# Rotary queries transposed by VectorE, the short weight tiles' low parts made by GpSimd, and scores one tile later

## What is computed

```python
q = (rms_norm(c_q, norm_cq) @ w_uq).reshape(B, S, MLA_HEADS, QK_NOPE + QK_ROPE)   # 16 heads, 128 + 64
q = jnp.concatenate([q[..., :QK_NOPE], apply_rope(q[..., QK_NOPE:], cos, sin)], axis=-1)
kv = (rms_norm(c_kv, norm_ckv) @ w_ukv).reshape(B, S, MLA_HEADS, QK_NOPE + V_HEAD)
k = jnp.concatenate([k_nope, jnp.broadcast_to(k_r, ...)], axis=-1)
o = chunk_causal_attention(q, k, v, (QK_NOPE + QK_ROPE) ** -0.5)
...
merged = jax.nn.sigmoid(gate_a) * y_a + jax.nn.sigmoid(gate_b) * y_b
x = x + merged @ w_o[l]
x = x + memory_cross_attention(rms_norm(x, norm_cross[l]), mem_n, ...)
x = x + swiglu(rms_norm(x, norm_ffn[l]), w_gate[l], w_up[l], w_down[l])
```

## Time and profile before

| what | value |
|---|---|
| median of 3 runs | 1653.96 us (1653.91 to 1654.84) |
| the profiled execution | 1653.59 us |
| its span, first to last instruction | 1651.8 us |
| mean granted TensorE clock | 0.998 |
| TensorE (PE) busy | 1640.0 us, 99% |
| TensorE weight loads (PEld), beside the products | 1372.2 us, 83% |
| VectorE (DVE) busy | 1199.7 us, 73% |
| ScalarE (ACT) busy | 812.0 us, 49% |
| GpSimd (POOL) busy | 105.2 us, 6% |

### The profile page before, as it was taken

One profiled execution on the slowest core, in us unless ns is written; L12 is line 12 of the kernel. 1 busy time (PEld: TensorE's weight loads), 2 busy tenths in 40 slices (PEclk: granted clock), 3 DMA queues, 4 the chain that ended last, 5 costly groups with the idle time before them and its releaser, 6 DMA issues.

```text
span 1651.8 us, 23135 instructions
## 1 busy us (share of the span) xinstructions
PE 1640.0 (99%) x7708; PEld 1372.2 (83%) x7708; DVE 1199.7 (73%) x1670; ACT 812.0 (49%) x1040; POOL 105.2 (6%) x154
## 2 busy tenths in 40 slices
PE   9999999999999999999999999999999999999998
PEld 7888888888888888888888888888888888888886
DVE  5678998899988877888668766666666666654454
ACT  7556554555444544555555544444444444344343
POOL 3100111120000000120002100000000000000000
PEclk9999999999999999999999999999999999999999
DMA  6875655555566675655435666666666666665564
GB/s 232 257 203 169 178 155 166 170 164 179 164 187 204 202 230 169 200 195 175 151 116 192 199 195 191 191 192 193 194 193 184 186 202 197 195 218 180 186 212 135
DMA packets 161408, 309.86 MB, mean 188 GB/s; under 512 B 10272, under 2 KB 16928, under 8 KB 161088
## 3 DMA queue, kind: packets, MB, share of 16 engines
q1 hardware_dynamic: 159152, 302.03, 59.7%
q0 software_dynamic: 1488, 6.42, 1.1%
q10 hardware_dynamic: 704, 0.58, 0.1%
HBM read 306.89 MB, written 2.10 MB: 187 GB/s over the span
## 4 chain that ended last, share of the span: by engine, by line
PE 98%; issue 0%; ACT 0%; DMA 0%; DVE 0%; SPq 0%; POOLq 0%; POOL 0%; ACTq 0%; DVEq 0%
PE acc L370 30%; PE acc L372 29%; PE acc L371 29%; PE tp L382 1%; PE sc L531 1%; PE acc L611 1%; PE acc L613 1%; PE acc L612 1%; PE ov L510 0%; PE sc L526 0%; DMA xs<-in_x_dram 0%; PE sc L499 0%; PE acc L460 0%; PE acc L461 0%; PE acc L462 0%
## 5 line engine op out<-in xcount | busy, mean ns | idle before, releaser
L1431 DVE TENSOR_TENSOR w_lo<-raw,w_hi 128x1024 fp32r<-128x1024 f32 (+3 forms) x591 | 719.5, 1222 | 345.8 <-ACT w_hi L856 337.9
L856 ACT ACTIVATE w_hi<-raw 128x1024 fp32r<-128x1024 f32 (+3 forms) x591 | 605.6, 1027 | 732.1 <-PE acc L372 681.8
L370 PE MATMUL acc<-w_hi,crossT 128*128 128x512 f32 x832 | 324.4, 390 | 0.2 <-ACTq L1119 0.2
L371 PE MATMUL acc<-w_lo,crossT 128*128 128x512 f32 x832 | 323.8, 389 | 0.0
L372 PE MATMUL acc<-w_hi,crossT 128*128 128x512 f32 x832 | 323.8, 389 | 0.0
L370 PE MATMUL acc<-w_hi,mixT 128*128 128x512 f32 x732 | 289.1, 395 | 1.4 <-DVE mixT L1642 1.2
L372 PE MATMUL acc<-w_hi,mixT 128*128 128x512 f32 x732 | 285.1, 390 | 0.0
L371 PE MATMUL acc<-w_lo,mixT 128*128 128x512 f32 x732 | 285.1, 389 | 0.0
L370 PEld LDWEIGHTS acc<-w_hi,crossT 128*128 128x128 f32 x832 | 156.2, 188 | 33.3 <-DVE w_lo L1431 0.5
L372 PEld LDWEIGHTS acc<-w_hi,crossT 128*128 128x128 f32 x832 | 156.2, 188 | 32.5
L371 PEld LDWEIGHTS acc<-w_lo,crossT 128*128 128x128 f32 x832 | 156.2, 188 | 32.0
(11 more groups left out here) (291 smaller groups left out, 1605.5 us busy)
## 6 DMA issues: line engine op xcount, KB each, us to landing
raw<-in_w_in_dram SPq DMA_DIRECT2D x104, 512.0 KB, 3.7
raw<-in_w_gate_dram SPq DMA_DIRECT2D x88, 512.0 KB, 4.3
raw<-in_w_up_dram SPq DMA_DIRECT2D x88, 512.0 KB, 3.7
raw<-in_w_down_dram SPq DMA_DIRECT2D x80, 512.0 KB, 4.6
raw<-in_w_kv_mem_dram SPq DMA_DIRECT2D x64, 512.0 KB, 3.7
raw<-in_w_o_dram SPq DMA_DIRECT2D x32, 512.0 KB, 4.4
raw<-in_w_q_mem_dram SPq DMA_DIRECT2D x32, 512.0 KB, 4.4
raw<-in_w_o_mem_dram SPq DMA_DIRECT2D x32, 512.0 KB, 4.0
```

The costliest lines, as they stand in the source:

```text
L370: mm(o, lo, whi, start=first and k == 0, stop=False)
L371: mm(o, hi, wlo, start=False, stop=False)
L856: fn(w_hi[:, s, 0:width], raw[:, s, 0:width], ACT.Copy).then_inc(hi_done, 1)
L1431: V.tensor_tensor(w_lo[:, s, 0:width], raw[:, s, 0:width], w_hi[:, s, 0:width].bitcast(F32), ALU.subtract).then_inc(lo_done, 1)
```

## The change

- TensorE no longer transposes rotary queries in the first seven pairs (`rotary_turned` is gone, and `rotary_out` on ScalarE). VectorE does it in 16 more transposes of 32 partitions by 64 elements, eight at step 3 and eight at step 4, behind a wait for `rope_ready`; the last of them now raises `q_turned`.
- The low parts of tiles 8 to 11 of every pair are made by GpSimd (`short_tiles_lo`, ahead of the rope). VectorE leaves its four splits out, waits for GpSimd's semaphore `pool_lo` one step later (steps 5 to 8), and raises `lo_done` in its place, so that `lo_done` is still counted in order.
- Values and scores stand after tile 7, not after tile 6; the masking and the gating on VectorE move to steps 7 and 8.
- The taps are shared out anew over the steps; their number is the same.
- Memory group 2 is made at step 10 of the last pair, not at step 11, on ScalarE ahead of the exponentials.
- GpSimd computes the memory's row factor after the first pair's rope.

```diff
-            def rotary_turned(p, q):
-                pe.wait_ge(rope_ready, p + 1)
-                for b in range(NB):
-                    turn_group(q, b, [qr_tok[:, b, :, :].rearrange("p h d -> p (h d)")])
...
-                if t == (4 if last else 6):
+                if t == (4 if last else 7):
                     if nth > 1:
                         values(i - 2, v_pair[parity], nth == 2)
-                    scores(i - 1, i + (Q_C - 1), nth == 1, last)
+                    scores(i - 1, nth == 1, last)
...
-            def rotary_out(p, q, first):
-                if not first:
-                    act.wait_ge(scores_ready, 2 * p)
-                for b in range(NB):
-                    act.wait_ge(turned, 2 * q + (b + 1))
-                    fn(qrT[:, b * P:(b + 1) * P], tp[:, b, 0:P], ACT.Copy).then_inc(turned_out[b], 1)
...
-                    if last and t == 11:
+                    if last and t == 10:
                         act.wait_ge(tile_done, i * 12 + (T_C + 8))
                         operand_hi(2)
...
             def query_turn(n):
-                i, j = n // 4, n % 4
+                i, j = n % 16 // 4, n % 4
+                if n >= 16:
+                    src = qr_tok[32 * i:32 * i + 32, :, j // 2, 32 * (j % 2):32 * (j % 2) + 32]
+                    to = qrT[32 * j:32 * j + 32, :].rearrange("p (b t) -> p b t", b=NB)
+                    ins = V.transpose(to[:, :, 32 * i:32 * i + 32], src)
+                    if n == 31:
+                        ins.then_inc(q_turned, 1)
+                    return
...
-                if t == (4 if last else 6):
+                if t == (4 if last else 7):
                     masked_scores(i - 1, nth == 1)
-                if t == (5 if last else 7) and nth > 1:
+                if t == (5 if last else 8) and nth > 1:
                     gate_values(i - 2)
...
-            share = [0, 1, 3, 5, 8, 10, 12, 12, 13, 16, 18, 19, EARLY_TAPS]
+            share = [0, 1, 3, 5, 6, 7, 9, 12, 12, 15, 18, 19, EARLY_TAPS]
-            share_last = [0, 1, 3, 5, 9, 12, 15, 15, 16, 17, 18, 19, EARLY_TAPS]
-            turn_now = {0: (7, 10), 1: (10, 13), 2: (13, 16)}
+            share_last = [0, 1, 3, 5, 6, 7, 9, 12, 12, 15, 18, 19, EARLY_TAPS]
+            turn_now = {0: (7, 10), 1: (10, 13), 2: (13, 16), 3: (16, 24), 4: (24, 32)}
...
-                    split_lo(i * 12 + T_C, t + 4, width)
+                    if t in (5, 6, 7, 8):
+                        dve.wait_ge(pool_lo, 4 * i + (t - 4))
+                        dve.sem_inc(lo_done, 1)
+                    if t not in (4, 5, 6, 7):
+                        split_lo(i * 12 + T_C, t + 4, width)
...
-                    if last and t == 11:
+                    if last and t == 10:
                         operand_lo(2)
...
+                    if t == 3 and not first:
+                        dve.wait_ge(rope_ready, i)
...
+            def short_tiles_lo(p):
+                for t, n in ((8, 2 * UQ), (9, 2 * UQ), (10, CH), (11, CH)):
+                    s = t % RING
+                    gp.wait_ge(hi_done, p * 12 + (T_C + t + 1))
+                    G.tensor_tensor(w_lo[:, s, 0:n], raw[:, s, 0:n], w_hi[:, s, 0:n].bitcast(F32), ALU.subtract)\
+                        .then_inc(pool_lo, 1)
+
             def query_rope(p, first):
+                short_tiles_lo(p)
                 gp.wait_ge(q_ready, 2 * p + 2)
                 if not first:
-                    gp.wait_ge(turned, 2 * p + 2 * Q_C)
+                    gp.wait_ge(q_turned, p)
```

More of the change, by code:

```diff
@@ L61 @@
 C_A, C_B, C_C, C_E, C_D, C_F, C_G, C_H, C_I, C_J = 0, 2, 6, 30, 38, 42, 46, 50, 54, 76
-Q_X, Q_CQ, Q_CKV, Q_B, Q_C, Q_LAST = 0, 4, 5, 6, 7, 14
-Q_D, Q_F, Q_G, Q_H = 15, 19, 20, 22
+Q_X, Q_CQ, Q_CKV, Q_B, Q_LAST = 0, 4, 5, 6, 7
+Q_D, Q_F, Q_G, Q_H = 8, 12, 13, 15
 H_X, H_CQ, H_CKV, H_D, H_F, H_G, H_H = 0, 8, 10, 11, 19, 21, 25
@@ L226, in program @@
         g_ready, u_turned, u_ready, tanh_done = (sem(n) for n in ("g_ready", "u_turned", "u_ready", "tanh_done"))
+        pool_lo = sem("pool_lo")
         q_ready, q_turned, kv_ready = sem("q_ready"), sem("q_turned"), sem("kv_ready")
@@ L512, in values, with scores @@
                 ins.then_inc(pv_done, 1)
-            def scores(p, q, first, last=False):
-                operand_ready(q)
-                if not last:
+            def scores(p, first, last=False):
+                if last:
+                    operand_ready(Q_LAST)
+                else:
                     pe.wait_ge(q_turned, p + 1)
@@ L539, in attention @@
                     if last:
-                        queries_turned(i - 1, i + (Q_C - 1))
-                    else:
-                        rotary_turned(i - 1, i + (Q_C - 1))
+                        queries_turned(i - 1, Q_LAST)
                     if nth > 1:
                         probs_turn(i - 2)
-                if t == (4 if last else 6):
+                if t == (4 if last else 7):
                     if nth > 1:
                         values(i - 2, v_pair[parity], nth == 2)
-                    scores(i - 1, i + (Q_C - 1), nth == 1, last)
+                    scores(i - 1, nth == 1, last)
             def gate_and_pair(i, nth, parity=0):
@@ L1040, in attention @@
                     if last:
-                        queries_out(i - 1, i + (Q_C - 1), False)
-                    else:
-                        rotary_out(i - 1, i + (Q_C - 1), nth == 1)
+                        queries_out(i - 1, Q_LAST, False)
                     if nth > 1:
@@ L1557, in query_turn @@
             def query_turn(n):
-                i, j = n // 4, n % 4
+                i, j = n % 16 // 4, n % 4
[6 more added lines that the diff above has]
+                    return
                 src = q_tok[32 * i:32 * i + 32, :, :, 32 * j:32 * j + 32]
                 to = qnT[32 * j:32 * j + 32, :, :].rearrange("p h (b t) -> p b h t", b=NB)
-                ins = V.transpose(to[:, :, :, 32 * i:32 * i + 32], src)
-                if n == 15:
-                    ins.then_inc(q_turned, 1)
+                V.transpose(to[:, :, :, 32 * i:32 * i + 32], src)
             def taps(j, w0, w1, before, turns=()):
@@ L2229, in _ @@
                 load_memory(c)
-            row_factor(R_MEM)
             gp.wait_ge(kr_ready, 1)
             gp.wait_ge(turned, 2 * Q_CKV + 2)
+            def short_tiles_lo(p):
[4 more added lines that the diff above has]
+                        .then_inc(pool_lo, 1)
             def query_rope(p, first):
+                short_tiles_lo(p)
                 gp.wait_ge(q_ready, 2 * p + 2)
                 if not first:
-                    gp.wait_ge(turned, 2 * p + 2 * Q_C)
+                    gp.wait_ge(q_turned, p)
                 q = [q_tok[:, :, :, NOPE + 32 * k:NOPE + 32 * k + 32] for k in range(2)]
@@ L2242, in _ @@
             query_rope(0, True)
+            row_factor(R_MEM)
             with gp.Fori(1, PAIRS) as i:
```

## The result

The changed kernel takes 1682.07 us in the median (1681.36 to 1682.47, four runs); the kernel before took 1653.93 on the same chip (1653.15 to 1654.84, four runs). The ratio is 1.0169 [1.0156, 1.0182]. 28.1 us were lost, where the prediction had 20.8 lost.

The account below looks back on a forecast made before the run. TensorE, busy 1640.0 of 1651.8 us, bounds the kernel, with VectorE nearest behind in the head pairs. 7.0 + 1.5 + 15.0 - 1.5 - 1.2 = +20.8 us gave 1675 us, range 1662 to 1691.

Parts of the forecast that it names:

- a sign of VectorE being late at another place: Sign of a wrong forecast: TensorE's gaps stand before products waiting for w_lo instead; the price may be either side.
- VectorE keeps up: Rival: transposes and holds cost no more than about 3 us a loop, so only 2.7 us gained: 1651.3 us, chance 0.08.
- All is held: Rival: transposes held too, or every subtraction meets a split; loops 6.4 us late, +42 us, 1696 us, chance 0.12.
- GpSimd slower than in proportion: Case: GpSimd's subtractions take 1.9 and 1.3 us, meeting more taps, 1.5 us more a loop: 1684; within main forecast's 0.72.
- Part 3: VectorE's list: 2.9 us spared, sixteen transposes at 0.245 us added (3.9); steady loop 33.9 us against TensorE's 33.3.
- Part 4: GpSimd's subtractions hold VectorE's splits and taps but let transposes pass; steady loop 36.3 us, 3.0 late per pair.
- five loops: Steady loops of pairs 3 to 7, each 36.3 us and 3.0 late: 15 us lost in all.
- 1.65 + 0.5 + 0.3: Holds on VectorE per steady pair: tile 8's subtraction 1.65 us, tile 9's 0.5, the rope's small operations 0.3.
- the tap behind the first eight transposes, about 0.5: Steady pair: tile 9's subtraction falls on the first eight short transposes and holds VectorE's next tap about 0.5 us.
- Pair 2: Unrolled pair: eight gaps of 0.18 us between VectorE's taps taken as gone, 1.5 us late.
- Pair 1: VectorE, delayed since pair 0, ends its transposes at 195.8; TensorE's scores, due at 188.8, are 7.0 us late.
- Parts 1 and 2: Gains on TensorE: 1.5 us from rotary transposes taken away in seven pairs, 1.2 from the earlier third memory group.

Follow-up runs that it names:

- neither part: Changed kernel, but TensorE transposes the rotary queries again and VectorE makes all low parts; later scores, new tap sharing and earlier memory group stay: 1654.04 us, ratio 0.9999.
- the transposes alone: Changed kernel, but VectorE again makes the low parts of tiles 8 to 11 and GpSimd does only the rope: 1665.87 us, ratio 1.0074.
- GpSimd's subtractions alone: Changed kernel, but TensorE transposes the rotary queries again and ScalarE copies them out; GpSimd keeps the four subtractions: 1663.30 us, ratio 1.0056.
- no reading by GpSimd: Changed kernel, but GpSimd subtracts only two columns of tiles 8 to 11 and fills the rest with zeros, leaving those low parts out: 1657.77 us, ratio 1.0023.
- the waits filled: Changed kernel with five extra 128x128 identity products on TensorE ahead of the wait for the sixteenth transpose, in seven pairs: 1677.17 us, ratio 1.0143.

## Why the prediction was right, and where its size was off

The runs add up as follows. With neither part 1654.0; the transposes alone +11.8; GpSimd's subtractions alone +9.3; both +28.0. The 7 us over the sum of the two are mostly the 4.9 of the clock: in the profiled executions of the parts alone it did not fall in the pairs. In the second no wait stands before the scores; in the first the longest is 2.15 us, which was near enough to a fall that luck has a part in it.

- **Direction and place: right.** The waits stand before the 64-row score products, released by a VectorE transpose of `qrT`, the largest in pair 1. Beside these 12.1 us stand 6.8 for `w_lo`, which the prediction had named as a sign of VectorE being late at another place: both places occur. VectorE is the bound of this stage. *VectorE keeps up* is out: the kernel is slower even with no reading by GpSimd, 1657.8. *All is held* is out, by the undisturbed transposes. *GpSimd slower than in proportion* named a time close to the measured one, 1684. Its durations came true (the subtractions that met little took 1.26 to 1.40 and 1.97 to 2.01 us), its 1.5 us more a loop did not: without the clock's share the loops are 0.6 over the forecast. That it came near 1682 is luck, since 4.9 us of the difference are TensorE's clock.
- **Part 3: right.** A transpose of 64 took 236 ns, eight 1.97 to 1.99 us: 0.245 each, as taken. With the holds gone the steady loop was 34.1 us, forecast 33.9.
- **Part 4: right in kind, small in size.** Without the clock's share the last five loops were 36.9 us in the mean (35.42, 37.59, 36.70, 37.45, 37.24), forecast 36.3. The holds are 36.9 - 34.1 = 2.8 a pair, where 1.65 + 0.5 + 0.3 = 2.45 stood. Tile 8's 1.65 was measured as 1.6. The term that was short is *the tap behind the first eight transposes, about 0.5*, for tile 9. In pairs 4, 6 and 7 tile 9's subtraction came early enough to catch the tap ahead of the transposes, 1.6 us each; in pair 5 it came later, ran back to back with tile 10's, and they held the tap behind for 0.85; in pair 3 it was 0.1. The mean is 1.15, and with tile 8's 1.6 that is the 2.8. With the 0.2 by which the loop without holds was longer, five loops were 17.9 us and not 15.0 over their 33.3. Pair 2 gave 0.75 (35.67 less the clock's 1.62 is 34.05, over 33.3) where 1.5 stood.
- **Pair 1: the total right by some luck, the place only in part.** The scores began at 195.83; forecast 195.8. Tile 12's low part began at 166.60, forecast 165.7. But 0.8 us of it were there before GpSimd's first subtraction: the split ahead of the gating began at 152.25, where it was 151.44, behind waits in the first 50 us that differ from execution to execution. So the change cost 6.3 there where 7.0 was forecast. And of the 7 us only 2.64 stand as a wait before the scores. TensorE had already stood at other places, two of which are these rows of its timeline:

```profile
161.88 0.41 PE L605 MATMUL acc<-w_hi,cqT 128*128 128x384 f32 x1 [1.14 <-DVEq L1652]
...
190.18 0.50 PE L371 MATMUL acc<-w_hi,mixT 128*128 128x512 f32 x1 [0.63 <-DVE w_lo L1415]
```

L1652 is the word that VectorE passes on for tile 8, which is queued behind its taps; the prediction saw that queue for the load of tile 12 and not for the tile's own products. These waits did not add to the 7.0, as far as the trace tells: TensorE stood once more, 2.64 us, behind them, so VectorE's chain was the later one.

- **Missing: the clock.** The sum took every wait at its own length. Three of them cost 1.6 us more each behind their end, 4.9 us by the trace, and with the waits filled the falls were gone. This is the largest single part of the 7.3 us by which the forecast was short.
- **Costed at nothing, and not nothing:** the later scores and the moved taps, 0.9 us by the loops of the kernel with both parts undone. In the changed kernel this is no term of its own, since its loops are counted whole above.
- **Parts 1 and 2: right within what can be told.** From pair 7's scores to pair 8's it was 30.11 us before and is 26.41 now. Of the 3.70, 2.73 are tile 7, which stands ahead of pair 7's scores and not of pair 8's; 0.97 are left, where 1.2 was forecast for the group (pair 7's two rotary transposes stood ahead of its scores, outside this stretch). The group alone, on the kernel before, gave 1.5 there.

Together: pair 1 7.1 (0.8 of it from before the change acts), pair 2 0.75, five loops 17.9, the clock 4.9, less 1.7 for part 1 (1.5, and 0.2 from the rounding of 33.3) and 1.0 at the end: about 27.9; the eighth scores begin at 445.56 and began at 417.66, which is 27.9 too. From there on only the offset is left.

None of these versions is faster than the kernel before by more than can be told; the memory group alone (0.9993 [0.9983, 1.0002]) is the one part that costs nothing.

## What to carry to other kernels

When one engine is at 98% and the next at 90% of a stage, count the second one's work from deadline to deadline before giving it anything, and count what a helper costs it: here a subtraction of 768 columns on GpSimd held a two-input instruction of VectorE for up to 1.6 us, so that sparing VectorE 2.9 us a pair shortened the loop by 1.3 (35.4 to 34.1) and lengthened it by 2.8 again. A new wait on TensorE may be paid once more behind its end, in half clock, as eleven waits of 1.89 to 3.37 us were here; look at the granted clock right behind every new wait, not at the mean over the span. Before two kernels of like times are called alike, take the clock's share out of both. Move the meeting points with care: taking tiles 8 and 9 back put tile 10's subtraction onto a split.

## What the runs showed of the hardware

- At eleven waits, of 1.89, 2.00, 2.03, 2.23 (twice), 2.27, 2.33, 2.41, 2.64, 3.16 and 3.37 us, TensorE's clock fell to its 1.2 GHz level; at waits of 2.04, 2.15, 2.19 and 2.21 us it did not, so the length of the wait alone does not decide. The fall came between 0.7 us before the end of the wait and 1.3 us behind it. At the ten of them that stand before scores it cost 1.6 us, once 2.9. With 1.28 us of idle products put into the wait the clock stayed full in all seven pairs. The Trainium skill ("TensorE: Matmul & The Clock Gate", section HAM oscillation — how this bites in real kernels) describes the same loss behind waits for data that come back at every tile; the waits here are for another engine.
- A product of two 128x128 float32 operands shows as two records, 24 for 12 instructions, at 0.12 us each.
- A fill by GpSimd left VectorE's two-input taps alone (0.48 us), a subtraction of 768 columns held them for up to 1.6 us; transposes of 64 elements per partition, 236 ns each, were held by neither.
